# Weight pieces loaded from ScalarE's DMA queue, and their maxima taken in the middle of VectorE's step

## What is computed

```python
h = rms_norm(x, p['norm1_w']) * (1.0 + sc1) + sh1
proj = h @ p['w_in']
# per chunk of 128 tokens, S carried from chunk to chunk
s = jnp.einsum('bhtd,bhsd->bhts', qc, kc) * inner
o = (jnp.einsum('bhts,bhse->bhte', s, vc)
     + jnp.einsum('bhtd,bhde->bhte', qc * qdec[..., None], S))
S = cdec[:, None, None] * S + jnp.einsum('bhsd,bhse->bhde', kc * kdec[..., None], vc)
y_r = head_norm(_merge(o_r), p['ret_norm_w'], R_HEADS) * jax.nn.silu(rg)
```

## Time and profile before

| | us |
|---|---|
| median of 3 runs | 2862.22 (2860.45 to 2865.99) |
| profiled execution, its own time | 2870.42 |
| its span, first to last instruction | 2868.6 |
| TensorE busy | 2580.2 (90%) |
| VectorE busy | 1677.5 (58%) |
| ScalarE busy | 793.4 (28%) |
| GpSimd busy | 397.3 (14%) |

### The profile page before, as it was taken

The page is one execution under the profiler, slowest core; times in us unless marked ns, Lnnn a source line. Parts: engine busy times, 40 slices in busy tenths (PEclk is TensorE's granted clock), DMA queues, the critical chain, the costliest instruction groups (busy, mean ns, idle before and its releaser), DMA issues. The chain is left out here.

```text
span 2868.6 us, 44774 instructions
## 1 busy us (share of the span) xinstructions
PE 2580.2 (90%) x17400; PEld 1570.8 (55%) x17400; DVE 1677.5 (58%) x3305; ACT 793.4 (28%) x1145; POOL 397.3 (14%) x389
## 2 busy tenths in 40 slices
PE   7798777996988999769969999999999987999998
PEld 1254444555776787635535666666666652444444
DVE  2646666753676776737875767766667765222222
ACT  1222222220443544304442222222222224111110
POOL 0022212220000000001232222122222200000000
PEclk9899988996999999769989999999999998999999
DMA  9724444427102010043311111111111107332321
GB/s 327 211 91 169 140 170 176 172 71 245 33 23 85 27 58 24 20 140 130 132 66 45 61 60 56 57 41 59 57 57 59 60 31 257 93 104 69 104 69 46
DMA packets 192688, 279.31 MB, mean 97 GB/s; under 512 B 16017, under 2 KB 131265, under 8 KB 188755
## 3 DMA queue, kind: packets, MB, share of 16 engines
q1 hardware_dynamic: 192604, 278.19, 29.8%
HBM read 202.95 MB, written 75.21 MB: 97 GB/s over the span
## 5 line engine op out<-in xcount | busy, mean ns | idle before, releaser
L279 PE MATMUL d_po<-d_w,d_a_parts 128*128 128x512 f16 x704 | 268.6, 381 | 27.8 <-DVE d_w L2719 27.8
L280 PE MATMUL d_po<-d_w,d_a_parts 128*128 128x512 f16 x704 | 268.6, 382 | 0.0
L281 PE MATMUL d_po<-d_w,d_a_parts 128*128 128x512 f16 x704 | 268.4, 381 | 0.0
L2248 PE MATMUL py<-h_parts,wide_weights 128*128 128x384 f16 (+1 forms) x792 | 246.4, 311 | 17.9 <-DVE u_p L2384 17.9
L2249 PE MATMUL py<-h_parts,wide_weights 128*128 128x384 f16 (+1 forms) x792 | 246.2, 311 | 0.0
L2250 PE MATMUL py<-h_parts,wide_weights 128*128 128x384 f16 (+1 forms) x792 | 246.1, 311 | 0.0
L279 PE MATMUL prj<-w_heads,h_parts_t 128*128 128x512 f16 x512 | 197.7, 386 | 9.9 <-DVE h_parts_t L864 5.0
L280 PE MATMUL prj<-w_heads,h_parts_t 128*128 128x512 f16 x512 | 197.7, 386 | 0.0
L281 PE MATMUL prj<-w_heads,h_parts_t 128*128 128x512 f16 x512 | 197.2, 385 | 0.0
L279 PE MATMUL m_prj<-m_h,w_heads 128*128 128x128 f16 (+1 forms) x1088 | 179.2, 218 | 11.4 <-DMA m_h<-h_parts 10.1
L2706 DVE SCALAR_TENSOR_TENSOR d_out<-d_po,d_scale,g_p 128x1024 f32<-128x1024 f32 x16 | 20.5, 1284 | 287.5 <-PE d_po L281 287.5
(11 more groups left out here) (432 smaller groups left out, 5699.7 us busy)
## 6 DMA issues: line engine op xcount, KB each, us to landing
wa<-in_w_ada_dram SPq DMA_DIRECT2D x12, 2048.0 KB, 21.5
u_raw<-in_w_up_dram SPq DMA_DIRECT2D x44, 512.0 KB, 5.0
d_a<-act_cols SPq DMA_DIRECT2D x15, 1408.0 KB, 7.3
act_cols<-u_a SPq DMA_DIRECT2D x44, 384.0 KB, 2.4
win_raw<-in_w_in_dram SPq DMA_DIRECT2D x8, 2048.0 KB, 17.2
S_s<-in_w_up_dram SPq DMA_DIRECT2D x8, 1408.0 KB, 7.1
w_piece<-in_w_up_dram SPq DMA_DIRECT2D x8, 1408.0 KB, 8.6
d_raw<-in_w_down_dram SPq DMA_DIRECT2D x11, 1024.0 KB, 6.9
```

Source lines behind the costliest of these rows:

```text
L279: nc.tensor.matmul(out, left[0], right[0], start=(k == 0), stop=False)
L280: nc.tensor.matmul(out, left[0], right[1], start=False, stop=False)
L281: return nc.tensor.matmul(out, left[1], right[0], start=False, stop=last)
L2248: nc.tensor.matmul(out, left[0], right[0], start=(start and k == 0), stop=False, skip_group_check=True)
```

## The change

The pieces are requested by ScalarE on its own DMA queue, at the end of its step, behind `square(c+2)`; SyncE no longer issues or waits for them. `find_max` moves from the end of VectorE's step, behind `norm(c+2)` and `find_scale` or `cut_lo`, into the step, between `h_lo(c+1)` and `state(c-1)`. Which piece is reduced in which step stays, and so does the number of instructions on VectorE.

```diff
@@ SyncE
             norm.load_x(sp, x_rows[2], 2, P)
 
-            def load_pieces(j, first=False):
-
-                of, at = (up_pieces, j) if not isinstance(j, int) or j < UPIECES else (down_pieces, j - UPIECES)
-                for u in range(2):
-                    if not first:
-                        sp.wait_ge(s["piece_maxed"], 2 * j + u - 1)
-                    sp.dma_start(piece[u], of[bass.ds(2 * at + u, 1)].rearrange("o p n -> (o p) n")).then_inc(s[f"piece_in{u}"], 16)
-
...
-            load_pieces(0, True)
             step(1)
             with sp.Fori(0, 3) as b:
                 step(2 * b + 2)
-                load_pieces(2 * b + 1)
                 loads(2 * b + 3)
                 prep.store_parts(sp, b)
                 prep.load_raw(sp, b + 1)
                 save_y(2 * b + 2, P)
-                load_pieces(2 * b + 2)
             step(8)
-            load_pieces(7)
...
-            for j in range(UPIECES, 3 * UPIECES // 2):
-                load_pieces(j)
-                step(j + 2)
+            with sp.Fori(10, NCH - 2) as c:
+                step(c)
@@ ScalarE
+            def load_pieces(of, at, j):
+
+                for u in range(2):
+                    if not isinstance(j, int) or j:
+                        act.wait_ge(s["piece_maxed"], 2 * j + u - 1)
+                    act.dma_start(piece[u], of[bass.ds(2 * at + u, 1)].rearrange("o p n -> (o p) n")).then_inc(s[f"piece_in{u}"], 16)
+
             norm.square(act, 2, P)
             step(1, P, P, P, P, qs_p)
-            with act.Fori(0, 4) as b:
+            load_pieces(up_pieces, 0, 0)
+            with act.Fori(0, 3) as b:
                 step(2 * b + 2, P, P, P, P, qs_p)
+                load_pieces(up_pieces, 2 * b + 1, 2 * b + 1)
                 step(2 * b + 3, P, P, P, P, qs_p, lambda: prep.cut_hi(act, b))
-            with act.Fori(10, NCH - 2) as c:
+                load_pieces(up_pieces, 2 * b + 2, 2 * b + 2)
...
@@ VectorE
-            def step(c, T, Ta, Tn, Tnn, steps, mask, between=None):
+            def step(c, T, Ta, Tn, Tnn, steps, mask, between=None, pieces=False):
...
                 if Tn:
                     h_lo(c + 1, Tn)
+                if pieces:
+                    find_max(c - 2)
                 state(c - 1)
...
-                step(2 * b + 2, P, P, P, P, steps, mask_p, lambda: prep.find_scale(dve, b))
-                find_max(2 * b)
-                step(2 * b + 3, P, P, P, P, steps, mask_p, lambda: prep.cut_lo(dve, b))
-                find_max(2 * b + 1)
+                step(2 * b + 2, P, P, P, P, steps, mask_p, lambda: prep.find_scale(dve, b), True)
+                step(2 * b + 3, P, P, P, P, steps, mask_p, lambda: prep.cut_lo(dve, b), True)
             with dve.Fori(10, NCH - 2) as c:
                 steps = Steps(dve, s["steps"], base.n + (c - 1) * per)
-                step(c, P, P, P, P, steps, mask_p)
-                find_max(c - 2)
+                step(c, P, P, P, P, steps, mask_p, None, True)
```

More of the change, by code:

```diff
@@ L838, in step @@
                     norm.square(act, c + 2, Tnn)
+            def load_pieces(of, at, j):
[3 more added lines that the diff above has]
+                    act.dma_start(piece[u], of[bass.ds(2 * at + u, 1)].rearrange("o p n -> (o p) n")).then_inc(s[f"piece_in{u}"], 16)
             norm.square(act, 2, P)
             step(1, P, P, P, P, qs_p)
-            with act.Fori(0, 4) as b:
+            load_pieces(up_pieces, 0, 0)
+            with act.Fori(0, 3) as b:
                 step(2 * b + 2, P, P, P, P, qs_p)
+                load_pieces(up_pieces, 2 * b + 1, 2 * b + 1)
                 step(2 * b + 3, P, P, P, P, qs_p, lambda: prep.cut_hi(act, b))
-            with act.Fori(10, NCH - 2) as c:
+                load_pieces(up_pieces, 2 * b + 2, 2 * b + 2)
+            step(8, P, P, P, P, qs_p)
+            load_pieces(up_pieces, UPIECES - 1, UPIECES - 1)
+            step(9, P, P, P, P, qs_p, lambda: prep.cut_hi(act, 3))
+            load_pieces(down_pieces, 0, UPIECES)
+            with act.Fori(10, NCH - 3) as c:
                 step(c, P, P, P, P, qs_p)
+                load_pieces(down_pieces, c - 9, c - 1)
+            step(NCH - 3, P, P, P, P, qs_p)
             step(NCH - 2, P, P, P, NS, qs_p)
```

## The result

The changed kernel takes 2884.59 us (median of 4 runs, 2881.41 to 2889.66) against 2862.12 us before (2860.45 to 2865.99). The ratio is 1.0078, with a 95% interval of 1.006 to 1.0096: slower by 22.5 us, where 12 were forecast and 2882 was the top of the range. The profiled execution took 2884.88 us, with a span of 2883.1 us.

The account below looks back on a forecast made before the run. TensorE was taken to bound steps 11 to 14 (floor 26.06 us), the 2 MB block and late x the long steps. +15.1 - 4.2 - 4.1 = +6.8, plus 5.2 for the clock, gave +12: 2874 us, range 2863 to 2882.

Parts of the forecast that it names:

- The pair in steps 11 to 14: TensorE's steps 11 to 14: the two piece reductions delay `xn`, TensorE waits 3.77 us in each step, +15.1 us.
- moves by as much: Steps 11 to 14: `xn` comes 5.69 us later, as the state update does, against a slack of 1.99 us.
- at the same point as before: Steps 11 to 14: the rotation is not delayed, since VectorE does the same work behind the low part of h.
- The clock: Steps 11 to 14: idle time lowers TensorE's clock, 1.74 us a fall, in three of four steps, +5.2 us.
- Steps 3, 5, 7 and 9: Long steps: the reductions fill the wait for x, and `outputs` follow L256 0.95 us sooner; -4.2 us in sum.
- Steps 4, 6, 8 and 10: The reductions fill VectorE's wait for `outputs`; TensorE waits 3.2 us in all but wins 1.84 per step; -4.1 us.
- GpSimd's own 7 us: Long steps, behind the all-reduce: the 7 us before GpSimd's sine part stay whatever VectorE does.
- rival A: Long steps: GpSimd's wait ends with the reductions, 7.2 instead of 0.95 us won in four steps; 2849 us, chance 0.06.
- rival B: Steps 5, 7 and 9: x is as late as before, held by store and load; 6.1 us more, 2880; chance 0.12.
- a sign of being wrong: On ScalarE: its square still waiting 10 us for x would show the forecast wrong.
- rival D: ScalarE becomes late: DMA issues of 4 us or more delay the rotation; 2 us in twelve steps, beyond 2895; chance 0.04.

Follow-up runs that it names:

- Sine after `xn`: The changed kernel with one more wait: GpSimd's sine part waits until VectorE's `xn` is written; 2877.83 us, ratio 1.0064.
- half the pair: The changed kernel, but VectorE's steps 10 to 13 reduce only the first 1408 of 2816 columns of each piece; 2859.82 us, ratio 0.9992.
- middle only: VectorE's program as in the changed kernel, SyncE and ScalarE as in the kernel before, so SyncE requests the pieces; 2919.94 us, ratio 1.0209.

## Why the prediction was wrong

The sign, the places and the order of the terms were right; the sum was too small by 10 us. Three terms were wrong by about as much each: the wait in steps 11 to 14 by 3.7 us, the clock by 3.2, the long steps by 3.5. By its own steps:

- **The pair in steps 11 to 14, +15.1.** The wait was 18.8. The failing step is that `xn` "moves by as much", 5.69: in step 12 it started 5.64 us later and became 1.00 us longer, since its new time is that of GpSimd's sine part. So it ended 6.64 us later, and `turn_x` came 4.70 us later where 3.77 were forecast. The rotation did not come "at the same point as before" either: it started 0.65 us later, which TensorE did not feel. I checked what the moved instructions wait for, not what those behind them run beside. Sine after `xn` shows the cause.
- **The clock, +5.2.** I took a fall in three of four steps at the 1.74 us of the earlier trace rows. It fell in all four and cost 8.4, 2.1 each. The mechanism was right; the size came from one stretch. That the fall comes with the longer wait, half the pair shows: 0.6 us of idle time leave the clock at 1.00. In sine after `xn` 1.05 and 2.27 us still lower it in all four steps. Why one fall costs 1.4 us and another 2.8 was not tried.
- **Steps 3, 5, 7 and 9, -4.2.** They gave -0.7. L256 came where I put it in three of four; in step 7 it was 1.74 us late, for y's store and x. From the store's request to x's arrival it took 20.0, 24.2 and 20.3 us in steps 5, 7 and 9, where I had put 21. Behind L256 the outputs came in 25.5, 25.3, 24.9 and 25.3 us (40.31 less 14.81 into step 3, and so on), where I had 24.9: the sine part started up to 0.6 us later than I took. The stretch from `outputs` to the next step, with its low clock, took 0.6 us more in sum. Why the sine part varies was not tried.
- **Steps 4, 6, 8 and 10, -4.1.** Measured -4.6. The four waits that the forecast works out add up to 3.4, not 3.2, which makes its term -4.0.
- **GpSimd's own 7 us** stayed with the pair gone: they were 6.8 to 7.5 us (rival A fell). **x** came in time for VectorE in three steps of four (rival B fell, but for 0.9 us). I had named as a sign of being wrong that ScalarE's square still waits 10 us for x; it waited 8 to 12 us, of which VectorE felt at most 0.91, so the sign was badly chosen: what counts is when VectorE wants x. ScalarE was not late (rival D fell; its issues took 0.33 to 0.45 us).
- The terms add up to 21.8 us measured, and the medians differ by 22.5. The spans of the two profiled executions differ by 14.5 only. The start of step 2 lies 2.1 us later in the changed kernel's, at 186.7; two kernels that are the same up to there (sine after `xn`, half the pair) reach it at 183.6 and 182.6, so that is scatter. Behind step 14, where nothing was changed, the kernel before took 2234.6 us in its profiled execution and the ten others 2220.8 to 2228.1, the changed one 2225.2: the execution before was a long one there, by about as much as it lies above its median.

What the forecast did not see at all is that the earlier request was needed by the move. It took the pieces as landed. In the changed kernel they were, and middle only shows that this was worth 35 us: that part of the forecast held without having been worked out.

## What to carry to other kernels

Before work is moved on an engine, list for both places what it lies below: here the old place was below another engine's 7 us wait in VectorE's steps 2, 4, 6 and 8 and behind all that TensorE wanted next in steps 10 to 13, and the new one is ahead of it. Where the traces show TensorE's clock falling behind a wait, price the wait by more than its length (here 2.1 us on top of 4.3 of idle time), and look at what the delayed instructions now run beside. The late transfers here were cured by their place in the order of requests, not by a queue of their own.

## What the runs showed that I had not expected

- A wait of 4.3 us in two pieces, 1.08 and 3.26 us with the q and k transposes between, lowered TensorE's clock in all four steps and cost a further 1.4 to 2.8 us each; a wait of 0.6 us at the second place left it at 1.00.
- In steps 11 to 14 the same reduction pair costs nothing at the end of VectorE's step and 6.8 us in its middle; at half the length it costs 0.8.
- With the pair in the middle, the place of the pieces in the order of requests alone decided between 2920 and 2880 us; which engine issued them decided nothing that could be told.
